# H of both MLPs turned by block transposes and on-chip transfers

## Chip, cores, metric

One core of one Trainium2 chip runs the whole program. The metric is the device time in microseconds (us), median over the executions shown.

## What is computed

Two transformer blocks in a row over 256 tokens with D = 2048, all in float32. The first has a modulated norm, dilated attention beside a gated recurrence, and an MLP; the second has stick-breaking attention and an MLP. Both MLPs have the same form, cut to what matters here:

```
ff = jnp.square(jax.nn.relu(h2.astype(dt) @ w_ff1[l])) @ w_ff2[l]        # first block, 2048 -> 8192 -> 2048

def squared_relu_mlp(h, w_in, w_out):                                    # second block, same sizes
    return jnp.square(jax.nn.relu(h @ w_in)) @ w_out
```

## The kernel before

Every large product is made of three TensorE products of float32r halves: a weight chunk `raw` (1 MB: 512 rows by 512 columns) is split by ScalarE into `w_hi` (`split_hi`, L243) and by VectorE into `w_lo` (`split_lo`, L247), and `chunk` (L252 and after) issues 24 matmuls for it: 2 token halves of 128 x 4 row blocks x 3 (L257 to L259). There is one `raw`, `w_hi` and `w_lo` buffer for each of the four chunks j of a block B, so chunk j of block B+1 can be split only when chunk j of block B has been used (`chunk_done`).

An MLP is cut into 16 units U of 512 hidden columns; two MLPs give 32 units. `up(U)` is four chunks that accumulate H of 512 columns for 256 tokens in PSUM. ScalarE writes `RE = relu(PS)` (L852; L855 in the second MLP, with the row's scale), VectorE writes `SQ = relu^2` (L1469). H has tokens on the partitions and `down` needs hidden columns there, so it is turned: `turn_unit` on TensorE makes eight 128x128 products with the identity (`turn_group`, L1695) into PSUM banks 6 and 7, ScalarE's `turn` copies them into `H_hi` (L865), VectorE's `turn` writes the rest into `H_lo` (L1490). `down(U)` then makes four chunks, one for each 512 output columns, which VectorE adds to `ACC` or `X` (L1506).

The order on TensorE, written out by hand, is up(U+1), down(U), up(U+2), down(U+1), and so on: between the end of up(U) and the start of down(U) lie down(U-1) and up(U+1). The eight identity products of unit U stand after the second chunk of down(U-1), those of the first unit of an MLP inside up(U+1). On ScalarE and VectorE the `turn` of U stands after the second split of the block that follows down(U-1), ahead of the third:

```
def down(B, U, par, end=False):          # ScalarE
    for j in range(CH):
        if not end:
            split_hi(act, B + 1, j)
        if j == 1 and par is not None:
            turn(U + 1, par)
```

Each engine works its list in order, so whatever a `turn` waits for, the splits of chunks 2 and 3 of the next block wait behind it. In the first MLP TensorE twice makes four products for the second gate (`gate_rows`, L1962) between a `down` and the next `up`; they use banks 6 and 7 and wait for `h_lo` of the unit turned last. GpSimd has nothing to do in the MLPs: its list is small power operations (`power`, L609) and the clearing of `ACC` (L615). Weights are loaded by SyncE, each when its `raw` buffer is free.

Of the kernel before, what the change touches and what calls it, by code (L numbers as in the profile page):

```python
# [28 lines left out]
F32 = mybir.dt.float32  # L29
# [93 lines left out]
LEVELS = (1, 2, 4, 8, 16)  # L123
WIDTHS = (0, 1, 2, 4, 8, 16, 32, 64, 128)
# [5 lines left out]
def build(nc, a, out):  # L130
    ctx = ExitStack()
    with ctx:
# [56 lines left out]
        Y0 = raw[:, 2:4, :, :].rearrange("p j k n -> p j (k n)")  # L189
        VN = V1[:, :, 0:NC_]  # L190
# [23 lines left out]
        relu_rdy, sq_rdy, h_tr, h_hi, h_lo, acc_read = (sem(n) for n in ("relu_rdy", "sq_rdy", "h_tr", "h_hi", "h_lo", "acc_read"))  # L214
# [220 lines left out]
        def _(sp):  # L435
# [70 lines left out]
            def mlp(M, w1, w2, gates):  # L506
# [73 lines left out]
        def _(pool):  # L580
# [33 lines left out]
            for t in range(T):  # L614
                pool.memset(ACC[:, t, :], 0.0).then_inc(acc_read, 1)  # L615
            with pool.Fori(MIX_JOBS + 2, JOBS) as i:
                power(i)


        @block.scalar  # L620
        def _(act):
# [224 lines left out]
            def mlp(m, M):  # L846
# [85 lines left out]
        def _(dve):  # L932
# [530 lines left out]
            def mlp(m, M, total):  # L1463
                def square(U, pair):
                    dve.wait_ge(relu_rdy, U + 1)
                    if not isinstance(U, int) or U:
                        dve.wait_ge(h_tr, U)
                    other = RE[:, :, :] if m else PS[:, pair:pair + 2, :]
                    dve.tensor_tensor(SQ[:, :, :], other, RE[:, :, :], ALU.mult).then_inc(sq_rdy, 1)  # L1469

# [16 lines left out]
                def turn(U, par):  # L1487
                    dve.wait_ge(h_hi, U + 1)
                    flat = "p k s -> p (k s)"
                    dve.tensor_tensor(H_lo[:, par, :, :].rearrange(flat), PS[:, 6:8, :],  # L1490
                                      H_hi[:, par, :, :].rearrange(flat).bitcast(F32), ALU.subtract).then_inc(h_lo, 1)
# [157 lines left out]
        def _(pe):  # L1649
# [279 lines left out]
            def mlp(m, M):  # L1929
                def up(B, U, turned=None, pair=0, turn_last=False):  # L1930
                    if turned is None and not turn_last:
                        pe.wait_ge(sq_rdy, U)
                    for j in range(CH):
# [3 lines left out]
                        if turn_last and j == 1:  # L1937
                            turn_unit(U - 1)

                def turn_unit(U):  # L1940
                    pe.wait_ge(sq_rdy, U + 1)
                    if not isinstance(U, int) or U:
                        pe.wait_ge(h_lo, U)
                    turn_group(SQ, 6).then_inc(h_tr, 1)

                def down(B, U, par, turn_next, mix=False):
                    pe.wait_ge(h_lo, U + 1)
                    for j in range(CH):
# [3 lines left out]
                        if j == 1 and turn_next:  # L1952
                            turn_unit(U + 1)
# [13 lines left out]
                up(M + 1, NU * m + 1, turn_last=True)  # L1967
                down(M + 2, NU * m, 0, True)
                for n, (i0, i1) in enumerate(MLP_LOOPS[m]):
                    with pe.Fori(i0, i1) as i:  # L1970
                        for e in range(2):
                            up(M + 3 + 4 * i + 2 * e, NU * m + 2 + 2 * i + e)
                            down(M + 4 + 4 * i + 2 * e, NU * m + 1 + 2 * i + e, 1 - e, True)
                    if m == 0 and n < 2:
                        gate_rows(n, 2 * i1 + 1)
                down(M + 2 * NU - 1, NU * m + NU - 1, 1, False, m == 0)
# [96 lines left out]
```

## Time and profile before

| | |
|---|---|
| median of two executions | 2431.09 us (2430.41 to 2431.77) |
| profiled execution, span from the first to the last instruction | 2431.4 us |
| TensorE busy | 2359.0 us, 97% of the span |
| VectorE busy | 1594.6 us, 66% |
| ScalarE busy | 1039.6 us, 43% |
| GpSimd busy | 51.4 us, 2% |
| DMA | 520.30 MB, mean 214 GB/s |

The profile is one execution. Busy time of an engine is the time in which it had an instruction; matmuls overlap, so how far apart they start says more than how long one lasts. The chain is followed back from the last instruction to whatever released each step; "idle before" is the time in which an engine waited, with what ended it.

### The profile page before, as it was taken

Reading aid. Unit: us, or ns where it says so; the run is one execution under the profiler, and the core shown is the slowest. Engines: PE = TensorE matmul, PEld = TensorE weight load, DVE = VectorE, ACT = ScalarE, POOL = GpSimd, SP = SyncE. Lnnn points to the kernel's source line nnn. Section 1 sums busy time; section 2 is a strip of 40 time slices with the busy share of each in tenths; the row PEclk is TensorE's granted clock in tenths of the full one; section 3 lists DMA queues with packets and bytes.
Section 4 is the critical chain, followed back from the end, with each engine's and each line's share of the span. In section 5 each row is a group of like instructions: output and inputs, shape, how many; then the busy total and the mean of one; then the engine's idle time right before and its main releaser. Section 6 shows DMA issues by size and latency. Waiting matters only on the chain.

```text
span 2431.4 us, 27934 instructions
## 1 busy us (share of the span) xinstructions
PE 2359.0 (97%) x10954; PEld 1968.0 (81%) x10954; DVE 1594.6 (66%) x1284; ACT 1039.6 (43%) x890; POOL 51.4 (2%) x56
## 2 busy tenths in 40 slices
PE   4899999999999999999999999999999999999999
PEld 3777888887888888888887888878888888888887
DVE  7868989987666666655568456556555565565554
ACT  2245553435333333333334556664443433433432
POOL 1011000001000000000000000000000000000000
PEclk9789999999999999999999999999999999999999
DMA  9988987755676776655554545444555655555552
GB/s 355 362 300 311 361 311 268 252 199 169 231 241 231 234 242 224 224 190 181 183 190 171 177 160 168 156 138 158 183 191 183 191 184 192 189 188 190 190 189 104
DMA packets 235129, 520.30 MB, mean 214 GB/s; under 512 B 9705, under 2 KB 10162, under 8 KB 232370
## 3 DMA queue, kind: packets, MB, share of 16 engines
q1 hardware_dynamic: 234352, 519.15, 63.2%
q8 instruction: 49, 0.80, 0.1%
q10 hardware_dynamic: 706, 0.17, 0.0%
q14 instruction: 22, 0.18, 0.0%
HBM read 517.19 MB, written 2.10 MB: 214 GB/s over the span
## 4 chain that ended last, share of the span: by engine, by line
PE 90%; DVE 4%; DMA 2%; ACT 2%; issue 1%; DVEq 1%; POOL 1%; ACTq 0%; SPq 0%
PE PS L257 28%; PE PS L259 28%; PE PS L258 28%; DMA ada_raw<-in_w_ada_dram 2%; PE PS L1695 2%; PE PS L1734 1%; PE PS L1669 1%; DVE w_lo L247 1%; PE PS L306 1%; ACT w_hi L243 1%; POOL rstd L609 1%; PE PS L1679 1%; DVE ada_acc L1144 0%; DVEq L1511 0%; PE PS L1799 0%
## 5 line engine op out<-in xcount | busy, mean ns | idle before, releaser
L247 DVE TENSOR_TENSOR w_lo<-raw,w_hi 128x2048 fp32r<-128x2048 f32 x392 | 897.6, 2291 | 688.4 <-ACT w_hi L243 683.4
L243 ACT ACTIVATE w_hi<-raw 128x2048 fp32r<-128x2048 f32 x392 | 750.9, 1916 | 1149.1 <-PE PS L259 1137.7
L257 PE MATMUL PS<-w_hi,A_hi 128*128 128x512 f32 x2112 | 839.7, 398 | 10.0 <-DVE A_lo L361 3.5
L259 PE MATMUL PS<-w_hi,A_lo 128*128 128x512 f32 x2112 | 827.5, 392 | 0.0
L258 PE MATMUL PS<-w_lo,A_hi 128*128 128x512 f32 x2112 | 827.2, 392 | 0.0
L257 PEld LDWEIGHTS PS<-w_hi,A_hi 128*128 128x128 f32 x2112 | 400.6, 190 | 92.2 <-ACT qT L738 2.8
L259 PEld LDWEIGHTS PS<-w_hi,A_lo 128*128 128x128 f32 x2112 | 399.5, 189 | 84.9
L258 PEld LDWEIGHTS PS<-w_lo,A_hi 128*128 128x128 f32 x2112 | 400.4, 190 | 81.2 <-issue 1.0
L257 PE MATMUL PS<-w_hi,H_hi 128*128 128x512 f32 x1024 | 401.6, 392 | 2.0 <-issue 1.3
L259 PE MATMUL PS<-w_hi,H_lo 128*128 128x512 f32 x1024 | 398.9, 390 | 0.0
L258 PE MATMUL PS<-w_lo,H_hi 128*128 128x512 f32 x1024 | 398.5, 389 | 0.0
L257 PEld LDWEIGHTS PS<-w_hi,H_hi 128*128 128x128 f32 x1024 | 192.3, 188 | 41.9 <-issue 2.2
L259 PEld LDWEIGHTS PS<-w_hi,H_lo 128*128 128x128 f32 x1024 | 192.2, 188 | 40.3
L258 PEld LDWEIGHTS PS<-w_lo,H_hi 128*128 128x128 f32 x1024 | 192.4, 188 | 38.9
L1144 DVE SCALAR_TENSOR_TENSOR ada_acc<-X,sc,ada_acc 128x1024 f32<-128x1024 f32 x90 | 115.3, 1281 | 4.5
L609 POOL TENSOR_TENSOR rstd<-ssq,mhalf 128x8 f32<-128x8 f32 x20 | 44.7, 2234 | 1666.3 <-DVE ssq L419 1399.8
L1506 DVE TENSOR_TENSOR ACC<-ACC,PS 128x1024 f32<-128x1024 f32 x60 | 72.8, 1214 | 0.0
L1506 DVE TENSOR_TENSOR X<-X,PS 128x1024 f32<-128x1024 f32 x60 | 72.8, 1213 | 0.0
L1089 DVE SCALAR_TENSOR_TENSOR MS<-ada_raw,sc,MS 128x2048 f32<-128x2048 f32 x25 | 58.8, 2350 | 14.8 <-DMA ada_raw<-in_w_ada_dram 14.1
L1669 PE MATMUL PS<-sc,ada_raw 128*128 128x1 f32 x160 | 29.9, 321 | 29.4 <-DMA ada_raw<-in_w_ada_dram 29.4
L1669 PEld LDWEIGHTS PS<-sc,ada_raw 128*128 128x128 f32 x160 | 29.8, 290 | 30.0 <-DMA ada_raw<-in_w_ada_dram 15.7
L1477 DVE SCALAR_TENSOR_TENSOR ada_acc<-gate_w,sc,ada_acc 128x2048 f32<-128x2048 f32 x16 | 37.6, 2352 | 4.0 <-issue 4.0
(267 smaller groups left out, 1108.0 us busy)
## 6 DMA issues: line engine op xcount, KB each, us to landing
raw<-in_w_ff_dram SPq DMA_DIRECT2D x128, 1024.0 KB, 5.3
raw<-in_mlp_w_in_dram SPq DMA_DIRECT2D x64, 1024.0 KB, 5.4
raw<-in_mlp_w_out_dram SPq DMA_DIRECT2D x64, 1024.0 KB, 5.0
raw<-in_w_in_dram SPq DMA_DIRECT2D x56, 1024.0 KB, 8.1
X<-in_w_ada_dram SPq DMA_DIRECT2D x96, 512.0 KB, 5.7
raw<-in_sb_w_qkv_dram SPq DMA_DIRECT2D x48, 1024.0 KB, 5.1
ada_raw<-in_w_ada_dram SPq DMA_DIRECT2D x32, 1024.0 KB, 9.8
raw<-in_w_out_dram SPq DMA_DIRECT2D x16, 1024.0 KB, 6.6
```

The source lines that it names most:

```text
L243: act.activation(w_hi[:, j, :, :], raw[:, j, :, :], ACT.Copy).then_inc(hi_rdy, 1)
L247: dve.tensor_tensor(w_lo[:, j, :, :], raw[:, j, :, :], w_hi[:, j, :, :].bitcast(F32), ALU.subtract).then_inc(lo_rdy, 1)
L257: pe.matmul(bank(pair + t), h, w_hi[:, j, k, :], start=first, stop=False)
L258: pe.matmul(bank(pair + t), h, w_lo[:, j, k, :], start=False, stop=False)
L259: mm = pe.matmul(bank(pair + t), l, w_hi[:, j, k, :], start=False, stop=last)
L609: pool.tensor_tensor(rstd[:, :], ssq[:, :], mhalf[:, :], ALU.pow).then_inc(rstd_rdy, 1)
L1089: ins = dve.scalar_tensor_tensor(out=MS[:, 1 - h, :], in0=sl, scalar=sc[:, k:k + 1], in1=MS[:, 1 - h, :], op0=ALU.mult, op1=ALU.add)
L1144: ins = dve.scalar_tensor_tensor(out=acc, in0=ada_ring[:, q % CH, :], scalar=sc[:, k:k + 1], in1=acc, op0=ALU.mult, op1=ALU.add)
L1477: dve.scalar_tensor_tensor(out=acc, in0=gate_w[:, half, :], scalar=c, in1=acc, op0=ALU.mult, op1=ALU.add).then_inc(gate_w_used, 1)
L1506: dve.tensor_tensor(ac, ac, PS[:, b:b + 2, :], ALU.add).then_inc(acc_read, 1)
L1669: mm = pe.matmul(bank(6, at, at + 1), ada_raw[:, k % CH, P * c:P * c + P], sc[:, k:k + 1], start=True, stop=True)
L1695: mm = pe.transpose(bank(first_bank + i, P * q, P * q + P), src[:, t, HD * h:HD * (h + 1)], ident[:, :])
```

## The change

TensorE makes no identity products for H any more. After the square, VectorE writes every 32x32 block of `SQ`, turned in itself, to the same place in `RE` (one instruction over 128x1024). Then each block stands turned but on the wrong group of 32 partitions and in the wrong column, and sixteen transfers from GpSimd, one for each pair of 32-partition groups (source a_, target q), move them from `RE` back to `SQ`: 32 partitions x 8 pieces of 32 float32 (128 bytes), 256 pieces and 32 KB each. ScalarE's `turn` waits until all sixteen have landed (four semaphores of four transfers) and reads `SQ` where it read PSUM; VectorE's `turn` likewise. The square of the next unit waits for `h_lo` where it waited for `h_tr`. SyncE's load loop of the second MLP has its first two rounds written out; the loads and their order are the same.

```diff
@@ on-chip buffers
+        SQ_flat, RE_flat = (x[:, :, :].rearrange("p t n -> p (t n)") for x in (SQ, RE))
+        SQ_to, RE_from = (x.rearrange("p (b q i) -> p b q i", q=P // BLK, i=BLK) for x in (SQ_flat, RE_flat))
+        SQ_turned = SQ_flat.rearrange("p (t k s) -> p k t s", t=T, k=CH)
@@ GpSimd, after the clearing of ACC (MLP 0), and after its last power loop (MLP 1)
+            def move_blocks(U):
+                pool.wait_ge(h_blk, U + 1)
+                for a_ in range(P // BLK):
+                    for q in range(P // BLK):
+                        pool.dma_start(SQ_to[BLK * q:BLK * (q + 1), :, a_, :],
+                                       RE_from[BLK * a_:BLK * (a_ + 1), :, q, :]).then_inc(h_in[q], 16)
+            for u in range(NU):
+                move_blocks(u)
             with pool.Fori(MIX_JOBS + 2, JOBS) as i:
                 power(i)
+            for u in range(NU, 2 * NU):
+                move_blocks(u)
@@ ScalarE, mlp
                 def turn(U, par):
-                    act.wait_ge(h_tr, U + 1)
-                    act.activation(H_hi[:, par, :, :].rearrange("p k s -> p (k s)"), PS[:, 6:8, :],
-                                   ACT.Copy).then_inc(h_hi, 1)
+                    for q in range(P // BLK):
+                        act.wait_ge(h_in[q], 16 * (P // BLK) * (U + 1))
+                    act.activation(H_hi[:, par, :, :].rearrange("p k (t s) -> p k t s", t=T), SQ_turned, ACT.Copy).then_inc(h_hi, 1)
@@ VectorE, mlp
                     if not isinstance(U, int) or U:
-                        dve.wait_ge(h_tr, U)
+                        dve.wait_ge(h_lo, U)
                     dve.tensor_tensor(SQ[:, :, :], other, RE[:, :, :], ALU.mult).then_inc(sq_rdy, 1)
+                    dve.wait_ge(sq_rdy, U + 1)
+                    dve.transpose(RE_flat, SQ_flat).then_inc(h_blk, 1)
@@ TensorE, mlp
-                def turn_unit(U):
-                    pe.wait_ge(sq_rdy, U + 1)
-                    if not isinstance(U, int) or U:
-                        pe.wait_ge(h_lo, U)
-                    turn_group(SQ, 6).then_inc(h_tr, 1)
-
-                def down(B, U, par, turn_next, mix=False):
+                def down(B, U, par, mix=False):
                     pe.wait_ge(h_lo, U + 1)
-                        if j == 1 and turn_next:
-                            turn_unit(U + 1)
```

On VectorE, inside the unit loop of the first MLP, from the square of a unit to its `turn` (`hi_rdy`: w_hi of a chunk is ready). Before:

```order
L1469 TENSOR_TENSOR SQ<-PS,RE 128x1024 [waits h_tr]
L246 ISA
L247 TENSOR_TENSOR w_lo<-raw,w_hi 128x2048 [waits hi_rdy]
L1506 TENSOR_TENSOR ACC<-ACC,PS 128x2x512
L246 REGISTER_ALU
L247 TENSOR_TENSOR w_lo<-raw,w_hi 128x2048 [waits hi_rdy]
L1506 TENSOR_TENSOR ACC<-ACC,PS 128x2x512
L1490 TENSOR_TENSOR H_lo<-PS,H_hi 128x1024 [waits h_hi]
L246 REGISTER_ALU
L247 TENSOR_TENSOR w_lo<-raw,w_hi 128x2048 [waits hi_rdy]
```

The same place after the change:

```order
L1488 TENSOR_TENSOR SQ<-PS,RE 128x1024 [waits h_lo]
L1490 STREAM_TRANSPOSE RE<-SQ 128x1024 [waits sq_rdy]
L251 ISA
L252 TENSOR_TENSOR w_lo<-raw,w_hi 128x2048 [waits hi_rdy]
L1527 TENSOR_TENSOR ACC<-ACC,PS 128x2x512
L251 REGISTER_ALU
L252 TENSOR_TENSOR w_lo<-raw,w_hi 128x2048 [waits hi_rdy]
L1527 TENSOR_TENSOR ACC<-ACC,PS 128x2x512
L1511 TENSOR_TENSOR H_lo<-SQ,H_hi 128x1024 [waits h_hi]
L251 REGISTER_ALU
L252 TENSOR_TENSOR w_lo<-raw,w_hi 128x2048 [waits hi_rdy]
```

One instruction has come in behind the square; the `turn` has kept its place, behind two splits and ahead of the third.

On GpSimd, the end of its list after the change (`h_blk`: the blocks of a unit are turned); before it had only the clearing, the powers and the branch:

```order
L628 DMA SQ<-RE 32x8x32 [waits h_blk]
L628 DMA SQ<-RE 32x8x32 x15
L628 DMA SQ<-RE 32x8x32 [waits h_blk]
L628 DMA SQ<-RE 32x8x32 x15
L133 UNCONDITIONAL_BRANCH
```

Sixteen transfers a unit have come in, the first of them behind one wait, the rest behind none; there are 512 in all.

## Rows read from the trace of the kernel before

**Rows 1.** The page's busy times, then its chain, shares of the span.

```profile
PE 2359.0 (97%) x10954; PEld 1968.0 (81%) x10954; DVE 1594.6 (66%) x1284; ACT 1039.6 (43%) x890; POOL 51.4 (2%) x56
...
PE 90%; DVE 4%; DMA 2%; ACT 2%; issue 1%; DVEq 1%; POOL 1%; ACTq 0%; SPq 0%
```

**Rows 2.** Busy time by stretch: the first MLP, the second.

```profile
602.00:1280.00 678.00, 676.11 (x3038) 559.13 (x3037) 430.58 (x242) 261.21 (x154) 0.00 (x0) 1.00 0.65 216
1740.00:2431.00 691.00, 686.93 (x3094) 569.45 (x3092) 385.95 (x217) 262.59 (x168) 0.00 (x0) 1.00 0.56 181
```

**Rows 3.** Timeline of TensorE (start us, us, engine, line) in one unit.

```profile
1804.46 0.39 PE L257 MATMUL PS<-w_hi,H_hi 128*128 128x512 f32 x1
...
1815.12 0.39 PE L259 MATMUL PS<-w_hi,H_lo 128*128 128x512 f32 x1
1815.35 1.03 PE L1695 MATMUL PS<-ident,SQ 128*128 128x128 f32 x8
1816.14 0.48 PE L257 MATMUL PS<-w_hi,H_hi 128*128 128x512 f32 x1
1816.45 0.40 PE L258 MATMUL PS<-w_lo,H_hi 128*128 128x512 f32 x1
1816.68 0.39 PE L259 MATMUL PS<-w_hi,H_lo 128*128 128x512 f32 x1
```

**Rows 4.** Instructions on tile SQ: duration ns min/median/max.

```profile
L1695 PE MATMUL PS<-ident,SQ x256: 270/273/273, 611.5 to 2393.7; 128*128 128x128 f32 x128
```

**Rows 5.** Timeline of VectorE, the same unit.

```profile
1806.61 2.29 DVE L247 TENSOR_TENSOR w_lo<-raw,w_hi 128x2048 fp32r<-128x2048 f32 x1 [3.15 <-ACT w_hi L243]
1808.82 1.22 DVE L1469 TENSOR_TENSOR SQ<-RE 128x1024 f32<-128x1024 f32 x1
```

**Rows 6.** Timeline of ScalarE, the same unit.

```profile
1804.66 1.92 ACT L243 ACTIVATE w_hi<-raw 128x2048 fp32r<-128x2048 f32 x1 [3.52 <-PE PS L259]
1806.48 1.25 ACT L855 ACTIVATE RE<-PS,rstd 128x512 f32<-128x512 f32 x2
...
1817.37 1.01 ACT L865 ACTIVATE H_hi<-PS 128x1024 fp32r<-128x1024 f32 x1
...
1827.31 1.92 ACT L243 ACTIVATE w_hi<-raw 128x2048 fp32r<-128x2048 f32 x1 [3.52 <-PE PS L259]
1832.75 1.92 ACT L243 ACTIVATE w_hi<-raw 128x2048 fp32r<-128x2048 f32 x1 [3.52 <-PE PS L259]
```

**Rows 7.** Instructions on tiles H_lo and rt: duration ns min/median/max.

```profile
L1490 DVE TENSOR_TENSOR H_lo<-PS,H_hi x32: 1215/1217/1219, 616.0 to 2398.4; 128x1024 fp32r<-128x1024 f32 x32
L1129 DVE STREAM_TRANSPOSE rt<-ada_acc x12: 711/711/712, 196.6 to 518.1; 128x512 f32<-128x512 f32 x12
```

**Rows 8.** DMA queues of the page (packets, MB, share), then issues with median us to landing.

```profile
q1 hardware_dynamic: 234352, 519.15, 63.2%
q10 hardware_dynamic: 706, 0.17, 0.0%
...
raw<-in_mlp_w_in_dram SPq DMA_DIRECT2D x64, 1024.0 KB, 5.4
wq_b<-in_q_norm_w_dram ACTq DMA_DIRECT2D x1, 64.0 KB, 4.4
rt<-in_positions_dram SPq DMA_DIRECT2D x2, 0.5 KB, 2.0
```

**Rows 9.** Timeline of ScalarE's queue and of GpSimd: one issue, one software instruction.

```profile
3.15 0.44 ACTq L624 DMA_DIRECT2D wq_b<-in_q_norm_w_dram  x1
...
1318.03 1.64 POOL L609 TENSOR_TENSOR rstd<-ssq,mhalf 128x8 f32<-128x8 f32 x1 [724.52 <-DVE ssq L419]
```

**Rows 10.** Second MLP: timeline of the first square, of TensorE at the first down.

```profile
1741.78 1.22 DVE L1469 TENSOR_TENSOR SQ<-RE 128x1024 f32<-128x1024 f32 x1
...
1760.02 0.39 PE L257 MATMUL PS<-w_hi,H_hi 128*128 128x512 f32 x1
```

**Rows 11.** The gate products of the first MLP, duration ns min/median/max.

```profile
L1962 PE MATMUL PS<-ada_acc,ones x8: 590/592/592, 1090.3 to 1182.2; 128*128 128x512 f32 x8
```

More of the change, by code:

```diff
@@ L123 @@
 LEVELS = (1, 2, 4, 8, 16)
+BLK = 32
 WIDTHS = (0, 1, 2, 4, 8, 16, 32, 64, 128)
@@ L213, in build @@
         gate_diag, gate_mm, gate_rdy = sem("gate_diag"), sem("gate_mm"), sem("gate_rdy")
-        relu_rdy, sq_rdy, h_tr, h_hi, h_lo, acc_read = (sem(n) for n in ("relu_rdy", "sq_rdy", "h_tr", "h_hi", "h_lo", "acc_read"))
+        relu_rdy, sq_rdy, h_blk, h_hi, h_lo, acc_read = (sem(n) for n in ("relu_rdy", "sq_rdy", "h_blk", "h_hi", "h_lo", "acc_read"))
+        h_in = [sem(f"h_in{q}") for q in range(P // BLK)]
         q_sig, f_rdy, g_sig, lv_wide = (sem(n) for n in ("q_sig", "f_rdy", "g_sig", "lv_wide"))
@@ L524, in mlp @@
                 up(M, 0)
-                first = KT // 2 + 1 if gates else 0
+                first = KT // 2 + 1 if gates else 2
+                up(M + 1, 1)
+                down(M + 2, 0)
+                up(M + 3, 2)
                 if gates:
-                    up(M + 1, 1)
-                    down(M + 2, 0)
-                    up(M + 3, 2)
                     gate_rows(0, 0)
-                    down(M + 4, 1)
+                down(M + 4, 1)
+                if gates:
                     gate_rows(1, 1)
@@ L1488, in turn @@
                     dve.wait_ge(h_hi, U + 1)
-                    flat = "p k s -> p (k s)"
-                    dve.tensor_tensor(H_lo[:, par, :, :].rearrange(flat), PS[:, 6:8, :],
-                                      H_hi[:, par, :, :].rearrange(flat).bitcast(F32), ALU.subtract).then_inc(h_lo, 1)
+                    by_token = "p k (t s) -> p k t s"
+                    dve.tensor_tensor(H_lo[:, par, :, :].rearrange(by_token, t=T), SQ_turned,
+                                      H_hi[:, par, :, :].rearrange(by_token, t=T).bitcast(F32), ALU.subtract).then_inc(h_lo, 1)
                 def gates(n):
@@ L1929, in mlp, with up @@
             def mlp(m, M):
-                def up(B, U, turned=None, pair=0, turn_last=False):
-                    if turned is None and not turn_last:
+                def up(B, U, turned=None, pair=0, second=False):
+                    if turned is None and not second:
                         pe.wait_ge(sq_rdy, U)
@@ L1966, in mlp @@
                     up(M, NU * m, 5, pair=pairs[2])
-                up(M + 1, NU * m + 1, turn_last=True)
-                down(M + 2, NU * m, 0, True)
+                up(M + 1, NU * m + 1, second=True)
+                down(M + 2, NU * m, 0)
                 for n, (i0, i1) in enumerate(MLP_LOOPS[m]):
@@ L1972, in mlp @@
                             up(M + 3 + 4 * i + 2 * e, NU * m + 2 + 2 * i + e)
-                            down(M + 4 + 4 * i + 2 * e, NU * m + 1 + 2 * i + e, 1 - e, True)
+                            down(M + 4 + 4 * i + 2 * e, NU * m + 1 + 2 * i + e, 1 - e)
                     if m == 0 and n < 2:
                         gate_rows(n, 2 * i1 + 1)
-                down(M + 2 * NU - 1, NU * m + NU - 1, 1, False, m == 0)
+                down(M + 2 * NU - 1, NU * m + NU - 1, 1, m == 0)
             def mix_turn(b):
```

2 lines of the change are left out of this document (removed).

## The prediction

> **What bounds the kernel now.** I read the busy times and the chain first [rows 1]: TensorE is busy for 97% of the span and is 90% of the chain that ended last, so time goes only where TensorE's list gets shorter or where it is made to wait. Then the two stretches of the MLPs [rows 2]: 676 of 678 us and 687 of 691 us, at the full granted clock (1.00, its 2.4 GHz level), with VectorE at 64% and 56%, ScalarE at 38%, GpSimd at nothing, the DMA engines at 65% and 56%. TensorE has no holes there: ScalarE's splits, each released by a finished chunk, come 5.44 us apart at 1827.31 and 1832.75 [rows 6]. That is a chunk's 24 matmuls at 0.227 us. A unit is eight chunks, 43.5 us, plus the identity products.
>
> **What is removed.** The eight identity products of a unit last 1.03 us [rows 3], 256 in all [rows 4], and sit between two matmuls that start at 1815.12 and 1816.14. That is 1.02 us instead of 0.23, so 0.79, and the next distance is 0.31 instead of 0.23, another 0.08: 0.87 us a unit. 32 units give **-27.8 us**, 1.1%. This is all that TensorE can give back, since each other matmul stays.
>
> **What is added beside TensorE.** VectorE gets 32 block transposes. A 128x512 one took 0.711 us [rows 7]; a column costs 1.05 ns, by the square's 1.22 us for 1024 and the split's 2.29 for 2048 [rows 5], so 1024 columns cost 0.71 + 512 x 1.05 ns = 1.25 us, 40 us in all in VectorE's idle time of 248 and 305 us [rows 2]. The copies into H_hi and H_lo read on-chip memory where they read PSUM; 1.01 us [rows 6] and 1.22 us [rows 7] are taken as they are, within 0.1 us (the square costs the same from either). SyncE's two rounds written out issue the same loads: nothing.
>
> **What is on the path.** The turning was hidden: down(U) stands two blocks behind up(U). Now it takes longer, so I follow one unit. TensorE ends up(U) and begins down(U-1) at 1804.46 [rows 3]. ScalarE splits from 1804.66, relu ends at 1807.73 [rows 6], VectorE's square runs 1808.82 to 1810.04 [rows 5], the block transpose then ends at 1811.3: 6.8 us after the end of up(U). Call L the time from there until the sixteen transfers have landed. ScalarE's `turn` waits for it, and behind it stands the split of chunk 2 of up(U+1), with VectorE's split behind that. From the start of `turn` to that chunk on TensorE: 1.01 + 1.92 (split) [rows 6] + 2.29 (split) [rows 5] + 0.2 of signals = 5.4 us; VectorE's 1.22 for H_lo fits beside ScalarE's split. TensorE wants chunk 2 after six chunks, at 1804.46 + 32.65 = 1837.1. So L may be 1837.1 - 5.4 - 1811.3 = **20.4 us**. Beyond that the loop is turn, 5.4, two chunks 10.9, then 6.8, then L: a period of 23.1 + L, and every us over 20.4 is paid.
>
> At six places there is less room. `down` of the last unit of each MLP follows directly on the down before it, and twice in the first MLP the gate products [rows 11] wait for the H_lo turned last, so H_lo must stand after four chunks: 1804.46 + 21.76 - 2.4 (1.01 + 1.22 + signals) - 1811.3 = **12.5 us** for L. The first unit of each MLP is alike: its square ends at 1743.0, transpose at 1744.25, and down begins at 1760.02, less 0.87 [rows 10]: 1759.15 - 2.4 - 1744.25 = 12.5. The other 28 steps from unit to unit have the 20.4. The change in time is therefore
>
> -27.8 + 6 x max(0, L - 12.5) + 28 x max(0, L - 20.4), which is 34 L - 674 beyond 20.4.
>
> It is zero at L = 17.1 and 2% (48.6 us) at L = 21.2.
>
> **L, which no row shows.** GpSimd issues nothing in this trace. One issue below: ScalarE's queue took 0.44 us for a transfer of 128 rows [rows 9]. Above: GpSimd's own small instruction on 128x8, worked by its software, took 1.64 us [rows 9]. GpSimd must make up 256 pieces for a transfer by software; I take it to be nearer to its own row, 1.25 us, an estimate two thirds of the way. Sixteen stand behind each other on one engine: 20.0 us. The last one's landing costs between 2.0 us (0.5 KB) and 5.4 us (1 MB among weights) [rows 8]; 64 KB took 4.4. I take 3.0. So L = 23.0, with ends 16 x 0.44 + 2.0 = 9.0 and 16 x 1.64 + 5.4 = 31.6.
>
> The Trainium skill weighs here too. Its page DMA: Bandwidth & Descriptors (section Anatomy of one DMA) gives a transfer issued by GpSimd a fixed cost of about 2.0 us, most of it the wait for the write's receipt, with descriptor making small, plus its bytes at 436 GB/s. If receipts overlap, an estimate by that page is 2.0 + 16 x 0.075 = 3.2 us for L and -27.8 us for the kernel; if each were waited for in turn, 16 x 2.075 = 33.2 us and about +455. The same page (Rules for kernel authors) says that transfers under 64 KB pay mostly overhead. The rows agree in kind: 64 KB took 4.4 us where 1 MB took 5.4 [rows 8]; no row shows a transfer from GpSimd.
>
> **Sum.** L = 23.0: 6 x 10.5 = 63.0, 28 x 2.6 = 72.8, less 27.8: +108. Against the profiled execution's 2431.4 us, which is 0.3 us over the median, that is **2539 us**, slower by 4.4%.
>
> **Rivals.**
> - *Hidden transfers, on the other side* (0.19): L stays under 17.1, that is under 0.88 us a transfer with a landing of 3. The threshold decides alone. For it: a hardware queue needs 0.44, GpSimd is free. Against: its software's 1.64. At 0.72 us, L = 14.5: -27.8 + 12 = -16, 2415 us; never under 2403.6. The skill's reading with overlapping receipts is this case.
> - *Between* (0.18): 0.88 to 1.14 us a transfer, L 17.1 to 21.2. What TensorE saves goes to the six tight places and a little more: 2431 to 2480, at L = 19 it is -27.8 + 39 = +11, 2443 us.
> - *My case* (0.47): L from 21.2 to 30, 2480 to 2780.
> - *The transfers queue in the DMA engines* (0.15): 4096 pieces a unit are 256 for each of 16 engines. A weight piece costs 0.632 x 16 x 2431.4 / 234352 = 0.105 us, a small one at most 0.028 (0.05% of the same on 706 packets) [rows 8]. If each small piece waits behind one weight piece: 256 x 0.133 = 34 us, and L = 37 with landing: 34 x 37 - 674 = +584, 3015 us. Against: with their own 256 weight pieces (27 us) the engines have 34 us of work in a period of 43.5, and weights are not always queued. A GpSimd that needs over 1.64 us a transfer ends here as well.
> - *No effect of the kind told* would need TensorE to keep a hole where the identity products stood (0.01, in "same" too).
>
> **Range and chances.** L from about 14 to 30 holds 8 in 10: 2412 to 2780. A measurement can tell about 2% from no change. Faster by over 2% would need -49 us where only 28 exist: 0.01. Within 2% are the first two rivals and what is left: 0.38. Slower: 0.61.
>
> **What the profile after would show.** No L1695 product of SQ, and a period of TensorE of 43.5 us where hidden, 23 + L (46) in my case. The sixteen transfers of a unit on GpSimd's queue, first start to last landing, are L. In the waits, ScalarE's `turn` waits for a DMA after the split of chunk 1 and TensorE's matmuls wait for w_lo of chunk 2; at the starts, ends and gates for H_lo. VectorE's transposes at 1.25 us. Wrong would be above all the 1.25 us a transfer: each 0.1 us is 54 us in the kernel, so size is much less sure than direction. The granted clock should stay at 1.00, as in [rows 2]; if the holes brought TensorE to its lower level of 1.2 GHz, the cost would be more than told.

## The result, and the profile after

The changed kernel takes 2507.51 us (2503.44 to 2511.57, 2 runs) against 2431.09: a ratio of 1.031, interval 1.029 to 1.033, 3.1% slower. I had forecast 2539 us, range 2412 to 2780. The profiled execution has a span of 2501.7 us against 2431.4, so 70.3 us have come in.

The page's busy times, GpSimd's DMA queue (packets, MB, share of 16 engines) and its chain, after:

```profile
PE 2357.8 (94%) x10698; PEld 1946.3 (78%) x10698; DVE 1626.7 (65%) x1316; ACT 1031.5 (41%) x890; POOL 350.2 (14%) x568
...
q0 software_dynamic: 16384, 16.81, 2.6%
...
PE 68%; issue 9%; DVE 7%; POOL 5%; DMA 3%; ACT 3%; DVEq 2%; ACTq 0%; SPq 0%; POOLq 0%
```

TensorE has 256 instructions fewer, but its busy time has hardly moved from that of [rows 1]: some of its matmuls run longer, as is seen below. Its part of the chain is down from 90% to 68%; GpSimd, "issue", the DMA engines and VectorE have come in. The kernel now waits for the turning of H.

Busy time by stretch, after, for both MLPs (stretch, length, then PE, PEld, DVE, ACT, POOL, each with its instructions, granted clock, DMA share, GB/s), to be laid beside [rows 2]:

```profile
602.00:1310.00 708.00, 662.27 (x2838) 536.78 (x2837) 427.45 (x245) 250.20 (x150) 142.82 (x245) 0.97 0.63 213
1775.00:2500.00 725.00, 708.33 (x3084) 579.32 (x3082) 417.51 (x253) 271.22 (x181) 150.92 (x257) 0.99 0.58 191
```

TensorE had 2 and 4 us without work in these stretches; now it has 46 and 17, and the granted clock is under 1.00. From the first square of an MLP to the next stage the first MLP takes 737.5 us (676.9 before), and from its first square to the end the second takes 699.4 (689.6): +60.6 and +9.8, which is all of the 70.

The waits, after (engine, line, what it waited for: us in total, times, longest):

```profile
ACT H_hi L885 <- DMA SQ<-RE: 477.8, 32, 17.7
...
POOL SQ L628 <- issue: 302.5, 178, 5.4
```

ScalarE's `turn` (L885) waits for the transfers in all 32 units, as told. The last row was not told: GpSimd, which should issue without a break, stands 178 times in the middle of its transfers, 302.5 us in all.

Tile SQ, after (duration ns min/median/max, first and last start), and the answer's line on landing:

```profile
L628 POOL DMA_DIRECT2D SQ<-RE x512: 582/582/752, 607.5 to 2464.2; - x171
...
L1490 DVE STREAM_TRANSPOSE RE<-SQ x32: 1245/1245/1247, 606.0 to 2451.3; 128x1024 f32<-128x1024 f32 x32
...
DMA to landing us min/median/max: 1.8/2.4/7.1
```

One unit of the second MLP: the block transpose on VectorE, the transfers on GpSimd, then `turn` on ScalarE (start us, us, engine, line; in brackets idle before, and what ended it):

```profile
1880.02 1.25 DVE L1490 STREAM_TRANSPOSE RE<-SQ 128x1024 f32<-128x1024 f32 x1
```

```profile
1881.66 1.75 POOL L628 DMA_DIRECT2D SQ<-RE  x3 [25.61 <-DVE RE L1490]
1885.09 1.76 POOL L628 DMA_DIRECT2D SQ<-RE  x3 [1.68 <-issue]
1890.38 1.75 POOL L628 DMA_DIRECT2D SQ<-RE  x3 [3.53 <-issue]
1895.70 1.75 POOL L628 DMA_DIRECT2D SQ<-RE  x3 [3.58 <-issue]
1897.88 1.75 POOL L628 DMA_DIRECT2D SQ<-RE  x3 [0.43 <-issue]
1899.98 0.58 POOL L628 DMA_DIRECT2D SQ<-RE  x1 [0.36 <-issue]
```

```profile
1901.95 1.06 ACT L885 ACTIVATE H_hi<-SQ 128x1024 fp32r<-128x1024 f32 x1 [14.55 <-DMA SQ<-RE]
```

The transpose ends at 1881.27 and `turn` starts at 1901.95: L = 20.7 us, and that is the median of the 32 units too (20.3 to 23.0, and 13.5 for the last, beside which hardly any weights are loaded). An issue is 0.58 us, so sixteen are 9.3 us; but they go in threes with 9.6 us of standing between them in this unit, and the last one lands 1.8 us after its issue starts.

At a tight place, the first `down` of the first MLP, TensorE after:

```profile
621.82 0.39 PE L264 MATMUL PS<-w_hi,A_lo 128*128 128x512 f32 x1
630.04 0.80 PE L262 MATMUL PS<-w_hi,H_hi 128*128 128x512 f32 x1 [7.84 <-DVE H_lo L1511]
630.64 0.63 PE L263 MATMUL PS<-w_lo,H_hi 128*128 128x512 f32 x1
...
634.90 0.51 PE L264 MATMUL PS<-w_hi,H_lo 128*128 128x512 f32 x1
635.25 0.40 PE L262 MATMUL PS<-w_hi,H_hi 128*128 128x512 f32 x1
```

The matmuls start 8.2 us apart instead of 0.23: a hole of 8.0 us, and L - 12.5 is 8.0 for this unit (its L is 20.5). Behind it twelve matmuls start 0.43 us apart, half speed, before the 0.23 comes back. The same place in two stretches of 4 us (columns as above; the granted clock is the third number from the end):

```profile
626.00:630.00 4.00, 0.00 (x0) 0.00 (x0) 1.23 (x1) 2.33 (x2) 0.29 (x1) 0.50 0.08 16
...
634.00:638.00 4.00, 4.00 (x16) 3.21 (x15) 3.44 (x3) 0.00 (x0) 0.13 (x1) 0.86 1.00 324
```

Just ahead it was 1.00. The clock falls to 0.50 (the 1.2 GHz level) in the hole and comes back 5 us after its end. Twelve matmuls in 4.9 us that would need 2.7 are 2.3 us, on top of the hole.

### The profile page after: what moved, and what is told of

The parts are those of the page before. It is cut to its first block, busy times and chain, and to the rows that moved or that the text cites. A ratio compares the mean times of both kernels' runs of the same rounds, so it can differ in the third digit from the quotient of the medians.

```text
span 2501.7 us, 27935 instructions
## 1 busy us (share of the span) xinstructions
PE 2357.8 (94%) x10698; PEld 1946.3 (78%) x10698; DVE 1626.7 (65%) x1316; ACT 1031.5 (41%) x890; POOL 350.2 (14%) x568
## 3 DMA queue, kind: packets, MB, share of 16 engines
q0 software_dynamic: 16384, 16.81, 2.6%
## 4 chain that ended last, share of the span: by engine, by line
PE 68%; issue 9%; DVE 7%; POOL 5%; DMA 3%; ACT 3%; DVEq 2%; ACTq 0%; SPq 0%; POOLq 0%
PE PS L262 21%; PE PS L264 21%; PE PS L263 21%; POOL SQ L628 5%; DVE w_lo L252 3%; DMA ada_raw<-in_w_ada_dram 2%; ACT w_hi L248 2%; DVEq L1494 2%; PE PS L1755 1%; DMA SQ<-RE 1%; PE PS L1690 1%; DVE RE L1490 1%; DVE SQ L1488 1%; POOL rstd L615 1%; PE PS L311 1%
## 5 line engine op out<-in xcount | busy, mean ns | idle before, releaser
L248 ACT ACTIVATE w_hi<-raw 128x2048 fp32r<-128x2048 f32 x392 | 741.2, 1912 | 745.3 <-PE PS L264 724.3
L262 PE MATMUL PS<-w_hi,H_hi 128*128 128x512 f32 x1024 | 408.8, 399 | 54.2 <-DVE ACC L1527 19.2
L628 POOL DMA_DIRECT2D SQ<-RE x512 | 298.8, 585 | 1109.0 <-DVE RE L1490 804.2
L263 PE MATMUL PS<-w_lo,H_hi 128*128 128x512 f32 x1024 | 404.3, 395 | 0.0
L264 PE MATMUL PS<-w_hi,H_lo 128*128 128x512 f32 x1024 | 404.0, 395 | 0.0
L1511 DVE TENSOR_TENSOR H_lo<-SQ,H_hi 128x1024 fp32r<-128x1024 f32 x32 | 39.2, 1225 | 403.2 <-ACT H_hi L885 403.2
L885 ACT ACTIVATE H_hi<-SQ 128x1024 fp32r<-128x1024 f32 x32 | 33.9, 1060 | 477.8 <-DMA SQ<-RE 477.8
L1108 DVE SCALAR_TENSOR_TENSOR MS<-ada_raw,sc,MS 128x2048 f32<-128x2048 f32 x25 | 58.8, 2350 | 13.5 <-DMA ada_raw<-in_w_ada_dram 13.0
```

The source lines that it names most:

```text
L248: act.activation(w_hi[:, j, :, :], raw[:, j, :, :], ACT.Copy).then_inc(hi_rdy, 1)
L262: pe.matmul(bank(pair + t), h, w_hi[:, j, k, :], start=first, stop=False)
L263: pe.matmul(bank(pair + t), h, w_lo[:, j, k, :], start=False, stop=False)
L264: mm = pe.matmul(bank(pair + t), l, w_hi[:, j, k, :], start=False, stop=last)
L628: pool.dma_start(SQ_to[BLK * q:BLK * (q + 1), :, a_, :], RE_from[BLK * a_:BLK * (a_ + 1), :, q, :]).then_inc(h_in[q], 16)
L1108: ins = dve.scalar_tensor_tensor(out=MS[:, 1 - h, :], in0=sl, scalar=sc[:, k:k + 1], in1=MS[:, 1 - h, :], op0=ALU.mult, op1=ALU.add)
```

## What the two traces leave open

L is 20.7, and for it the forecast's formula gives 34 x 20.7 - 674 = +30 us. The kernel lost 76. And the gap is uneven: unit to unit (`turn` to `turn`) the second MLP runs at 44.0 us, close to the 23.1 + 20.7 = 43.8 of the sum, while the first runs at 46.6 to 48.7 in its first eight units and at 55 in the two with gate products. So three questions: why GpSimd stands, what else costs time in the first MLP, and whether the 27.8 us removed were there at all.

**Theory.** GpSimd stands because the descriptions of its transfers have little room: the program reserves 1024 bytes for them (L2074). A transfer is 256 pieces, 16 for each of 16 engines. The Trainium skill, page DMA: Bandwidth & Descriptors (sections SWDGE vs HWDGE vs iDMA, and The descriptor swizzle), says that GpSimd writes descriptors into rings in on-chip memory, one for each piece and one more per engine for completion; section Why small descriptors are slow (HBM only) gives 16 bytes each. An estimate from that page of the Trainium skill, if the reserved bytes are those of one engine's ring: 17 x 16 = 272 bytes a transfer, so 1024 hold three. The trace agrees, three at a time. **Rival A:** each transfer is slow in itself, since GpSimd makes up 256 pieces by software. **Rival B:** the DMA engines are full of weights and land late. **Rival C:** ScalarE's hardware queue (0.44 us an issue, [rows 9]) would do the same work in less time.

## Experiments on the length of the turning

The runs of the kernel before that went with them were 2432.81, 2432.21 and 2432.95 us for the three groups (e1 to e4, e5 to e8, e9 to e12); ratios are against these.

**e1: 3328 bytes of room.** Three small tiles share memory with others to make the space; nothing else changes.

```diff
-        count, maskadd = sb("count", [P, 3 * P]), sb("maskadd", [P, 3 * P])
+        maskadd = sb("maskadd", [P, 3 * P])
...
-        wq_b, wk_b = sb("wq_b", [P, P]), sb("wk_b", [P, P])
+        w_b = sb("w_b", [P, 2 * P])
+        wq_b, wk_b, SEL = w_b[:, 0:P], w_b[:, P:2 * P], w_b[:, 0:7 * 32]
...
-        SEL = sb("SEL", [P, 7 * 32])
...
+        count = small[:, 512:896]
...
-    nc = bacc.Bacc("TRN2", target_bir_lowering=False, num_devices=1, dynamic_dma_scratch_size=1024)
+    nc = bacc.Bacc("TRN2", target_bir_lowering=False, num_devices=1, dynamic_dma_scratch_size=3328)
```

> The changed kernel with 3328 bytes a partition of room for transfer descriptions where it has 1024 (the tile count and the tile SEL share other tiles' memory, so that it fits). Theory A, the batches: three transfers fit into the room (17 descriptions a transfer and engine, 64 places), GpSimd issues three in 1.75 us and then stands until the room is free. With places for 12, L (end of the block transpose to the start of ScalarE's turn) falls from 20.7 us to 16 x 0.58 + 2.4 = 11.7 to 13 us, the period to 43.5 us, and the time to 2403 to 2412 us. Theory B, the DMA engines: the gaps are transfers that wait behind the weights' pieces, whatever room there is: L stays at 20 to 21 us and the time at 2500 to 2510 us.

2440.07 us (2431.21 to 2442.86), ratio 1.003 (1.002 to 1.004): 67 of the 76 us are gone. The way is that of theory A, the size is not: it said 2403 to 2412 us and an L of 11.7 to 13. In the profiled execution, which is the fastest of the six, L has a median of 15.1 (14 to 15.8 in most of the second MLP, 14.1 to 19.8 in the first). GpSimd in one unit of the second MLP, then in one of the first:

```profile
1814.91 6.91 POOL L629 DMA_DIRECT2D SQ<-RE  x12 [30.18 <-DVE RE L1491]
1824.52 2.30 POOL L629 DMA_DIRECT2D SQ<-RE  x4 [2.70 <-issue]
...
804.05 2.30 POOL L629 DMA_DIRECT2D SQ<-RE  x4 [29.77 <-DVE RE L1491]
810.48 5.17 POOL L629 DMA_DIRECT2D SQ<-RE  x9 [4.13 <-issue]
```

In the first of them twelve go out in one row, and the estimate from the Trainium skill has the same (3328 / 272 = 12.2). But it is not twelve in every unit. Counted through the whole kernel, the first stand comes after transfer 12 and the others after 21, 30, 39, 57, 75 and so on, each a multiple of nine later; where the row of a unit breaks depends on that count, six units have no break, and GpSimd stands 98 us in all. When it goes on, one to three of its transfers are still under way.

**e2: 2048 bytes** (as e1 with the other number).

> The same with 2048 bytes: 128 places, 7 transfers. Theory A: batches of 7, two stands of some 3 us, L 13 to 16 us, time 2405 to 2425 us. Theory B: as the changed kernel, 2500 to 2510 us.

2465.27 us (2460.98 to 2467.86), ratio 1.013 (1.011 to 1.014), L 16.6: both over theory A's (2405 to 2425 us, 13 to 16). One unit:

```profile
1895.53 6.42 POOL L629 DMA_DIRECT2D SQ<-RE  x11 [29.30 <-DVE RE L1491]
1904.59 2.32 POOL L629 DMA_DIRECT2D SQ<-RE  x4 [2.64 <-issue]
```

Eleven before the first stand here, where seven would fit at once. In the first unit of the kernel the stands come after transfers 7, 11 and 15, and from there on always at such a step of four.

**e3: 512 bytes** (one execution; the tiles lie as in the changed kernel).

> The changed kernel with 512 bytes: 32 places, one transfer at a time. Theory A: every transfer stands for the landing of the one before, 16 times 2.5 to 3.5 us, L 40 to 56 us, and by 34 L - 674 over the kernel before the time is 3100 to 3700 us. Theory B: no change, 2500 to 2510 us.

3217.05 us in one run. One transfer at a time: 2.1 to 2.2 us from start to start in most of a unit, up to 5.4 while weights are loaded:

```profile
1018.41 0.58 POOL L628 DMA_DIRECT2D SQ<-RE  x1 [1.55 <-issue]
1020.52 0.59 POOL L628 DMA_DIRECT2D SQ<-RE  x1 [1.52 <-issue]
```

L is 42 and the period 67 (23.1 + 42 = 65). Pieces, bytes, engines and queue are those of the other three; only the room differs (e1 and e2 also lay three tiles elsewhere). Put together, with the L of the last unit, beside which hardly any weights are loaded:

| room, bytes | L, median us | L of the last unit | 6 x (L - 12.5) + 28 x (L - 20.4) - 27.8 | measured |
|---|---|---|---|---|
| 512 | 42 | 34.9 | +754 | +784 |
| 1024 | 20.7 | 13.5 | +30 | +76 |
| 2048 | 16.6 | 10.8 | -3 | +32 |
| 3328 | 15.1 | 10.9 | -12 | +7 |

(a bracket below zero counts as zero.) The room moves L, and the formula with the median L comes out 19 to 46 us short of the time. That rest is the subject of the next part.

**e4: fewer pieces.** The same 32 KB a transfer as 32 pieces of 1 KB instead of 256 of 128 bytes. The blocks land in the wrong columns, so H is not the right one.

```diff
-                        pool.dma_start(SQ_to[BLK * q:BLK * (q + 1), :, a_, :],
-                                       RE_from[BLK * a_:BLK * (a_ + 1), :, q, :]).then_inc(h_in[q], 16)
+                        pool.dma_start(SQ_flat[BLK * q:BLK * (q + 1), 256 * a_:256 * a_ + 256],
+                                       RE_flat[BLK * a_:BLK * (a_ + 1), 256 * q:256 * q + 256]).then_inc(h_in[q], 16)
```

> The changed kernel with room of 1024 bytes, where each transfer moves 32 rows of 1 KB in one piece in place of 8 pieces of 128 bytes (the blocks land in the wrong columns, so H is not the right one; bytes and number of transfers are the same). Theory A: 3 descriptions a transfer and engine, so all 16 fit and there are no batches: L 11 to 13 us if an issue still costs 0.58 us, or 5 to 9 us if the issue itself gets cheaper with fewer pieces, time 2403 to 2410 us. Theory B: bytes are the same, the weights are the same: gaps stay, at least half of them, over 2450 us.

2426.36 us (2423.40 to 2429.49), ratio 0.998 (0.997 to 0.999). L has a median of 13.1. Theory A's 2403 to 2410 us is missed again, theory B's 2450 by more. Its tile SQ:

```profile
L628 POOL DMA_DIRECT2D SQ<-RE x512: 496/496/674, 607.1 to 2387.7; - x171
```

An issue costs 0.50 us with an eighth of the pieces, against 0.58. So rival A is false as I had it in the prediction: eight times the pieces cost 0.09 of 0.58 us. What the pieces cost is room: with fewer of them in the same 1024 bytes, GpSimd's standing falls from 302.5 us to 57.5. Theory A had no stand at all here, since by its estimate (3 x 16 = 48 bytes a transfer) all sixteen fit. The count is right for the first stand, which comes after transfer 21 (1024 / 48 = 21.3), and the others follow a multiple of eighteen later. So the room of a transfer that has landed is not had back at once: after the first stand the steps are three transfers shorter than the room (18 of 21, 9 of 12, 4 of 7). Why three, no run shows. That pieces are cheap to issue agrees with the Trainium skill, page DMA: Bandwidth & Descriptors, section Anatomy of one DMA, that many descriptors can be emitted before it shows.

**Rival B, the DMA engines,** has a part in L. The changed kernel's median landing of 2.4 us hides two kinds of transfers. In the unit shown above, nine were issued while weights were loaded and seven after that (each stretch with its DMA share, the number before the last, then the landing of the transfers issued in it):

```profile
1881.00:1895.00 14.00, 13.89 (x62) 11.12 (x61) 7.11 (x5) 2.89 (x2) 5.25 (x9) 1.00 0.72 235
DMA to landing us min/median/max: 2.4/4.3/5.0
...
1895.00:1902.00 7.00, 7.00 (x32) 5.82 (x31) 0.00 (x0) 0.05 (x1) 4.08 (x7) 1.00 0.15 33
DMA to landing us min/median/max: 1.8/1.8/1.9
```

The long stands (1.7, 3.5, 3.6 us) wait for the first kind, the short ones (0.4) for the second. The last unit of the kernel has the same room, and from 2456 us on hardly any weights beside it (DMA share 0.20):

```profile
2452.95 1.75 POOL L628 DMA_DIRECT2D SQ<-RE  x3 [25.07 <-DVE RE L1490]
2455.70 1.75 POOL L628 DMA_DIRECT2D SQ<-RE  x3 [1.01 <-issue]
```

There GpSimd stands 2.5 us in place of 9.6, and L is 13.5. The table has the same for the other rooms: 4 to 7 us less in the last unit. So the room decides whether GpSimd has to wait for landings, and the weights decide how long such a wait is: some 7 of the 20.7 us. This compares units of one execution; no run takes the weights away from the others.

**e8: ScalarE issues the sixteen transfers**, behind its first split of the block; its `turn` keeps its place behind the second.

```diff
-            def move_blocks(U):
-                pool.wait_ge(h_blk, U + 1)
...
+                def move_blocks(U):
+                    act.wait_ge(h_blk, U + 1)
+                    for a_ in range(P // BLK):
+                        for q in range(P // BLK):
+                            act.dma_start(SQ_to[BLK * q:BLK * (q + 1), :, a_, :],
+                                          RE_from[BLK * a_:BLK * (a_ + 1), :, q, :]).then_inc(h_in[q], 16)
...
+                        if j == 0 and par is not None:
+                            move_blocks(U + 1)
```

> The changed kernel with the sixteen transfers issued by ScalarE's queue, behind the first split of the next block, in place of GpSimd. Theory A (what costs is how the descriptions are made and where they are kept): 16 x 0.44 us behind a split that ends at +0.7 us, landing 2.4 to 4 us: L 10 to 12.5 us, no batches of three, time 2405 to 2420 us. Theory B (small pieces wait behind the weights' pieces in the DMA engines): L 17 us or more, time over 2440 us. Rival C: 7 us of issues on ScalarE hold up its splits of chunks 1 and 2: TensorE waits for w_lo, periods of 45 us and more with a short L.

2679.60 us (2678.69 to 2683.55), ratio 1.102 (1.100 to 1.104). L is 12.5, as theory A had it, and the kernel is the slowest but one, as rival C had it: periods of 52 to 55 us. ScalarE in one unit, then TensorE at the same place of another:

```profile
1950.66 10.55 ACTq L874 DMA_DIRECT2D SQ<-RE  x16
1961.33 1.91 ACT L248 ACTIVATE w_hi<-raw 128x2048 fp32r<-128x2048 f32 x1 [9.99 <-PE PS L264]
```

```profile
1914.39 0.79 PE L262 MATMUL PS<-w_hi,H_hi 128*128 128x512 f32 x1 [4.86 <-DVE X L1526]
```

An issue holds ScalarE for 0.66 us and sixteen for 10.6, in which it splits nothing. VectorE's split behind it is late, so is the add behind that, and TensorE waits for the add. The short L is there, the gain is not: an engine that others wait for can't spend 10 us on issues. Its queue also shows 139,970 packets. Less the 706 of [rows 8] that is 512 x 272: the 256 pieces of a transfer and sixteen more, one for each engine, which is the 17 an engine of the estimate above. GpSimd's queue shows 16,384 packets for the same transfers.

```profile
q10 hardware_dynamic: 139970, 16.98, 4.1%
```

## Experiments on what else the kernel lost

**e6: the sums for the second gate cut short.** In the first MLP, VectorE's list also has the sums for the gate (L1498), which I had left out. Ahead of the square, after:

```profile
764.13 2.35 DVE L1498 SCALAR_TENSOR_TENSOR ada_acc<-gate_w,sc,ada_acc 128x2048 f32<-128x2048 f32 x1 [0.20 <-issue]
766.40 4.49 DVE L252 TENSOR_TENSOR w_lo<-raw,w_hi 128x2048 fp32r<-128x2048 f32 x2
771.18 2.35 DVE L1498 SCALAR_TENSOR_TENSOR ada_acc<-gate_w,sc,ada_acc 128x2048 f32<-128x2048 f32 x1 [0.29 <-issue]
773.45 4.49 DVE L252 TENSOR_TENSOR w_lo<-raw,w_hi 128x2048 fp32r<-128x2048 f32 x2
777.85 1.22 DVE L1488 TENSOR_TENSOR SQ<-PS,RE 128x1024 f32<-128x1024 f32 x1
```

The split behind `turn` makes VectorE late, and here it must catch up through two rows of 2.35 us more, without a rest, before the next square. Once the loop turn, split, square, transfers, turn is closed, that lies on it.

```diff
-                    dve.scalar_tensor_tensor(out=acc, in0=gate_w[:, half, :], scalar=c, in1=acc,
+                    dve.scalar_tensor_tensor(out=acc[:, 0:8], in0=gate_w[:, half, 0:8], scalar=c, in1=acc[:, 0:8],
```

> The changed kernel where the gate sums of the first MLP (VectorE, L1498, 128x2048, two a unit) are made over 8 columns only (the second gate is wrong for it; loads and waits are the same). Theory A: after a late turn VectorE is busy without a break, and the two gate sums of 2.35 us lie in the loop of the first MLP: its periods fall from 46.8 to 44.0 us in eight to nine units, the time by 20 to 27 us to 2481 to 2488 us. Rival: the 2.8 us are the gate's weight loads, which take the transfers' place in the DMA engines: L would be longer in the first MLP; it is the same, so here nothing would change, 2503 to 2510 us.

2480.43 us (2478.82 to 2482.04), ratio 1.020 (1.018 to 1.022): 27 us back, with L unchanged at 20.7. Between the two profiled executions it is 23; the changed kernel's two executions lie 8 us apart. The first MLP's periods, 46.6 to 48.7 us before, are 43.5 to 45.9, near those of the second MLP. The sums are no news to VectorE; but in the kernel before TensorE had only 2 us without work in this stretch [rows 2], so there they cost no more than that.

**e7: the gate products don't wait for `H_lo`.** The second group of products waits instead until VectorE has read those of the first from the same banks.

```diff
-                    pe.wait_ge(h_lo, U + 1)
+                    if n:
+                        pe.wait_ge(gate_rdy, 4 + 2 * n)
```

> The changed kernel where the gate products no longer wait for h_lo of the unit turned last (banks 6 and 7 hold no H any more; they wait for the reader of the gate products before). Theory A: two of the six tight places go; their periods of 55 us fall to 44 or 45, time by 18 to 24 us to 2483 to 2490 us. Rival: the loop with 23.1 + L takes over at the same place and the late turn is paid a few chunks later: a fall by less than 10 us.

2486.36 us (2485.72 to 2488.10), ratio 1.022 (1.021 to 1.024): 21.2 us back, 17 between the two profiled executions; both are far over the rival's 10. The two periods of 55 become 46. The price of a tight place by the traces is some 8 us of hole and 2.3 of clock, near 21 us for two, which agrees as well as the changed kernel's 8 us between two executions lets one tell. In the changed kernel the gate product behind the hole:

```profile
1129.26 1.19 PE L1973 MATMUL PS<-ada_acc,ones 128*128 128x512 f32 x1 [7.65 <-DVE H_lo L1511]
```

**e5: no transfers.** ScalarE's `turn` waits for the block transpose alone, so that what was removed from TensorE is seen by itself. H stays unturned, so the result is not the MLP.

```diff
-            for u in range(NU):
-                move_blocks(u)
...
-            for u in range(NU, 2 * NU):
-                move_blocks(u)
...
-                    for q in range(P // BLK):
-                        act.wait_ge(h_in[q], 16 * (P // BLK) * (U + 1))
+                    act.wait_ge(h_blk, U + 1)
```

> The changed kernel without the 512 transfers: ScalarE's turn waits only for the block transpose and reads SQ as the square left it (H stays unturned, so what down computes is not the MLP). Theory A: what is left of the change is the identity products' going, 27.8 us, with VectorE's transposes hidden: 2401 to 2409 us. Rival: VectorE's 32 x 1.25 us show in part, because in the first MLP the gate sums stand beside them: 2412 us or more.

2418.70 us (2418.09 to 2419.73), ratio 0.994 (0.993 to 0.996): 13.5 us faster than before, half of the 27.8. The time is what the rival had (2412 us or more), but not for its reason: the period is 43.9 us, not 43.5, in both MLPs alike, with gate sums and without. TensorE where the identity products had stood, and VectorE beside it:

```profile
1808.64 0.39 PE L264 MATMUL PS<-w_hi,H_lo 128*128 128x512 f32 x1
1809.13 0.49 PE L262 MATMUL PS<-w_hi,H_hi 128*128 128x512 f32 x1
```

```profile
1805.57 2.29 DVE L252 TENSOR_TENSOR w_lo<-raw,w_hi 128x2048 fp32r<-128x2048 f32 x1 [0.73 <-ACT w_hi L248]
1807.78 1.22 DVE L1522 TENSOR_TENSOR X<-X,PS 128x1024 f32<-128x1024 f32 x1
```

Chunk 2 of `down` writes where chunk 0's result lies, and waits until VectorE has added it. That add stands behind a split and ends at 1809.00; TensorE would be ready at 1808.87 and starts at 1809.13. The 0.79 us of identity products stood in just this gap and hid it. Two starts, 0.49 and 0.33 instead of 0.23 each, are 0.37 us a unit.

**e9: as e5, with the add ahead of the split. e10: the kernel before with that same swap.**

```diff
-                        split_lo(dve, B + 1, j)
...
+                        dve.wait_ge(chunk_done, 4 * B + j + 1)
...
+                        split_lo(dve, B + 1, j)
```

> The kernel without transfers (H unturned, down computes something else) and, in down on VectorE, the add of a chunk ahead of the split that goes with it (it waits for the chunk itself). Theory A: without the identity products chunk 2 of each down stands 0.37 us for the add of chunk 0, which came behind a split; with the add first the period falls from 43.93 to 43.5 us and the time by 30 x 0.37 = 11 us to 2405 to 2411 us. Rival: the 0.37 us are TensorE's own (a long wait list at that chunk): unchanged, 2417 to 2420 us.

> The kernel before with the add first on VectorE, nothing else. Theory A: there the identity products cover the add, so nothing changes: 2428 to 2436 us, no more than 0.2% either way. Rival: the add first helps by itself, 2415 to 2425 us.

e9: 2405.65 us (2404.01 to 2405.74), ratio 0.989 (0.987 to 0.990), periods of 43.5: 27.3 us, which is the whole of the 27.8. e10: 2432.51 (2431.37 to 2435.21), ratio 1.000 (0.999 to 1.001): where the identity products cover the add, the swap is worth nothing.

## A version that beats both

**e11: room for twelve, gate products free, add first** (the edits of e1, e7 and e9 on the changed kernel, with its transfers).

> The changed kernel with room of 3328 bytes for descriptions, gate products that don't wait for h_lo, and the add first. Theory A: from the 2440 us with the room alone, two gate periods of 48 us fall to 43.5 (-9), 30 units lose 0.37 us (-11), and the loop of the first MLP is shorter by the add's place: 2412 to 2424 us, 0.3 to 0.9% under the kernel before. Rival: landings of 4 us beside weights keep L over 15 in the first MLP, TensorE's holes stay: 2425 us or more.

2417.13 us (2416.39 to 2421.06), ratio 0.994 (0.992 to 0.995), L 14.9: as expected.

**e12: as e11, and only twelve transfers.** The four pairs with source equal to target need no change of partitions; VectorE copies those blocks.

```diff
                     for q in range(P // BLK):
+                        if q == a_:
+                            continue
...
+                    for a_ in range(P // BLK):
+                        rows_ = slice(BLK * a_, BLK * (a_ + 1))
+                        dv = dve.tensor_scalar(SQ_to[rows_, :, a_, :], RE_from[rows_, :, a_, :], 0.0, None, ALU.add)
+                    dv.then_inc(h_diag, 1)
```

> As the kernel before this one, and the four blocks whose group of partitions stays the same (a_ = q) are copied from RE to SQ by VectorE (4 instructions of 32x256) in place of a transfer: 12 transfers a unit. Theory A: 12 fit into the room at once, issues last 7.0 us in place of 9.3, L falls by 2.3 to 4 us to 11 to 12.5 us, under the bound of the tight places: 2404 to 2414 us. Rival: VectorE's copies (4 x 0.4 us) push the split and the add of chunk 0 so late that TensorE waits there again: 2416 us or more.

2406.79 us (2404.58 to 2409.07), ratio 0.989 (0.988 to 0.991): 1.1% faster than before, 4% faster than the change as it was made. GpSimd in one unit of the second MLP, then both MLPs by stretch:

```profile
1887.00 2.88 POOL L631 DMA_DIRECT2D SQ<-RE  x5 [36.44 <-DVE RE L1494]
1890.04 4.03 POOL L631 DMA_DIRECT2D SQ<-RE  x7 [0.16 <-issue]
```

```profile
602.00:1280.00 678.00, 675.54 (x2971) 557.58 (x2970) 477.78 (x333) 265.28 (x159) 110.77 (x192) 1.00 0.68 228
1740.00:2406.00 666.00, 662.25 (x2922) 548.23 (x2920) 415.42 (x289) 259.42 (x165) 105.42 (x184) 1.00 0.60 195
```

In the second MLP GpSimd stands less than 1 us a unit and L is mostly 11 to 12 us. Nine units of the first MLP still have stands of 1.5 to 4 us and an L of 13.4 to 15.3, but they lie where 20.4 us are free. The median L is 11.7, TensorE is without work for 2.5 and 3.8 us, and the granted clock is 1.00 in both stretches. Turning by block transposes and transfers does give what TensorE saves; it needs L below 12.5 at the tight places and below 20.4 elsewhere.

## Why the prediction was right, point by point

- **The number:** slower was right and 2507.5 us lies in the range, but how near it came to 2539 is partly luck. L was taken 2.3 us too long, which is 78 us too much by 34 L - 674; what is missing from the sum is 46 us too little. With the right L the same sum says 2461 us.
- **What bounds the kernel, what is on the path:** right. A split waits behind `turn` in 28 steps, and there are six tight places. The hole at the first was 8.0 us, just L - 12.5. With L set to 42, the formula gave +754 and +784 was measured, and the periods were 67 where 23.1 + L says 65. The changed kernel's 44.0 in the second MLP is near 23.1 + 20.7 = 43.8, but shows nothing: without any transfers it is 43.9 there (e5).
- **"The sixteen stand behind each other on one engine: 20.0 us", at 1.25 us each:** the sum came out near, its parts did not. An issue is 0.58 us (9.3 for sixteen), nearer to the 0.44 of ScalarE's queue than to GpSimd's 1.64, and 9.6 us are GpSimd standing for want of room. The last landing was 1.8 and not 3.0. L = 20.7 instead of 23.0. That L falls in the rival I called "between" (17.1 to 21.2), for which the sum had 2431 to 2480 us; the time lies above that, for what is missing from the sum.
- **The rival "queue in the DMA engines":** not at its size (34 us of queueing, L of 37), but not nothing. Beside weights a transfer lands 4.3 us after its issue in the median, after them 1.8, and the last unit has an L of 13.5. By that comparison some 7 us of L are the weights', and they show as stands because the room is short.
- **The rival "hidden":** not here; with room for twelve, L falls to 15.1, and the loss is nearly gone (e1, +7 us); with twelve transfers and the two other edits it is true (e12).
- **Removed, -27.8 us:** the size was right (e9: -27.3), but not free: without a swap on VectorE half of it goes to the add of chunk 0 (e5: -13.5). I had asked what the identity products cost and not what they covered.
- **Missing from the sum, one:** VectorE's gate sums in the first MLP (e6: 27 us). I read the loop's free time in a unit of the second MLP and took it for both.
- **Missing from the sum, two:** at the last `down` of each MLP TensorE waits longer than for `H_lo`. The end of the first MLP, VectorE and TensorE:

```profile
1332.37 1.21 DVE L1527 TENSOR_TENSOR ACC<-ACC,PS 128x1024 f32<-128x1024 f32 x1
...
1333.69 0.76 PE L262 MATMUL PS<-w_hi,H_hi 128*128 128x512 f32 x1 [12.80 <-issue]
```

`H_lo` is ready at 1327.64, but the first chunk of this `down` writes where chunk 2 of the one before lies, and the add of that chunk stands on VectorE's list behind `H_lo`, two more additions and a split. The hole is 12.8 us where L - 12.5 says 7.8. At the end of the second MLP it is 4.5 where L - 12.5 says 1.0.
- **The granted clock "should stay at 1.00":** wrong. It fell to 0.50 in the long holes, and the twelve matmuls at half speed behind one cost 2.3 us, some 14 for the six.
- **VectorE's 1.25 us a transpose, ScalarE's and VectorE's `turn` from on-chip memory:** 1.245 us; 1.06 instead of 1.01 and 1.226 instead of 1.217. Right, and nothing.

The sum again, against the 70.3 us between the traces: +30 by the formula with L = 20.7; +27 gate sums (e6); +14 clock; -7 since the last L is 13.5; +7 at the two ends (5.0 and 3.5 beyond the formula, less the 1.3 that TensorE waited at the first of them before). That is 71. These are estimates that may overlap, and e6 alone is good to a few us, so the agreement is better than the parts. Three of the four terms added to the formula are read from the trace; only the gate sums have a run of their own. The 0.37 us of the add is not in the sum: the formula counts all 27.8 as gained, and that the add costs nothing where TensorE waits anyway is argued, not shown.

**Open.** Why L is longer in the first MLP once there is room (e12: mostly 14 to 15 against 11 to 12). The median landing is 4.5 us there against 2.5, the DMA share 0.68 against 0.60, and gate weights are loaded only there, but no run takes them away. What sets the steps of nine, four and eighteen transfers between stands is open too (in e12, with the room of e1, they are eight). Room for all sixteen was not tried.

## What to carry to other kernels

A step that is hidden today has a slack, and the slack differs by place: work it out for each, since moving work from TensorE to a slower path costs nothing up to the slack and a full microsecond for every one beyond it (28 such steps in a kernel here, and six places with less room). Before trusting what a removed instruction gives back, look at what it covered: the next thing on that engine's list may have been late all along. And count the transfers that are wanted at once from GpSimd before writing them: the room for their descriptions decides whether GpSimd must wait for landings, and with that whether sixteen go out in 9 us or in 40; the other loads of that moment decide how long each wait is.

## What the runs showed of the hardware

- GpSimd issues a transfer of 256 pieces of 128 bytes in 0.582 us and one of 32 pieces of 1 KB in 0.496. It goes on issuing only while there is room: the first stand comes after 1, 3, 7 and 12 transfers of 256 pieces with 512, 1024, 2048 and 3328 bytes, and after 21 of 32 pieces with 1024; later stands come at steps of 4, 9 and 18 for the last three.
- ScalarE's queue takes 0.66 us for the same 256 pieces (10.55 for sixteen), and ScalarE computes nothing in that time; its queue counts 272 packets a transfer.
- An on-chip transfer of 32 KB in 128-byte pieces lands 1.8 us after its issue where the DMA share is 0.15; beside weights, at 0.72, it took 2.4 to 5.0 us, 4.3 in the median.
- A hole of 8 us on TensorE brings the granted clock from 1.00 to 0.50, and the twelve matmuls behind it start 0.43 us apart instead of 0.23.
- A block transpose of 128x1024 float32 on VectorE takes 1.245 us, 0.711 for 128x512.
